# A two-layer transformer block on one core: mean of squares ahead of the input sums, head squares in smaller pieces, fifth product in another bank

## Time and profile before

| | us |
|---|---|
| median of three runs | 1791.35 (1790.88 to 1792.32) |
| profiled execution | 1793.69 |
| its span, first to last instruction | 1792.0 |
| PE busy | 1772.9 (99%) |
| DVE busy | 1279.3 (71%) |
| ACT busy | 895.0 (50%) |
| POOL busy | 140.7 (8%) |
| mean granted TensorE clock, share of full | 0.996 |

### The profile page before, as it was taken

One profiled execution on the slowest core, in us unless ns is written; L12 is line 12 of the kernel. 1 busy time (PEld: TensorE's weight loads), 2 busy tenths in 40 slices (PEclk: granted clock), 3 DMA queues, 4 the chain that ended last, 5 costly groups with the idle time before them and its releaser, 6 DMA issues.

```text
span 1792.0 us, 26289 instructions
## 1 busy us (share of the span) xinstructions
PE 1772.9 (99%) x8791; PEld 1500.4 (84%) x8791; DVE 1279.3 (71%) x1689; ACT 895.0 (50%) x1248; POOL 140.7 (8%) x190
## 2 busy tenths in 40 slices
PE   9999999999999999999999999899999999999999
PEld 7888888888888888888888887677888888888887
DVE  6567777556898788878877868887888655555654
ACT  7434444446455455545544556566544455554442
POOL 1012121000001000000000000110003011000000
PEclk9999999999999999999999999999999999999999
DMA  9564545555568667766775676455655655555554
GB/s 331 201 218 158 169 159 176 183 170 188 177 208 237 196 192 213 232 186 191 217 234 187 201 230 203 139 187 188 200 187 177 199 176 177 175 176 188 188 188 153
DMA packets 99116, 347.30 MB, mean 194 GB/s; under 512 B 11472, under 2 KB 11872, under 8 KB 98656
## 3 DMA queue, kind: packets, MB, share of 16 engines
q1 hardware_dynamic: 93392, 333.23, 57.0%
q0 software_dynamic: 4784, 12.60, 3.3%
q10 hardware_dynamic: 864, 0.44, 0.1%
HBM read 336.77 MB, written 2.11 MB: 189 GB/s over the span
## 4 chain that ended last, share of the span: by engine, by line
PE 90%; DVE 4%; ACT 3%; issue 2%; DMA 2%; POOL 0%; SPq 0%; ACTq 0%; DVEq 0%; POOLq 0%
PE bank L472 30%; PE bank L451 23%; PE bank L456 12%; PE bank L766 6%; PE bank L768 6%; PE bank L767 6%; DMA raw<-in_stream 2%; ACT w_hi L978 2%; DVE w_lo L1486 1%; PE bank L522 1%; PE bank L488 1%; ACT gate L1366 1%; PE bank L644 1%; PE bank L659 1%; PE bank L601 0%
## 5 line engine op out<-in xcount | busy, mean ns | idle before, releaser
L1486 DVE TENSOR_TENSOR w_lo<-raw,w_hi 128x1024 fp32r<-128x1024 f32 x620 | 754.5, 1226 | 386.7 <-ACT w_hi L978 382.9
L978 ACT ACTIVATE w_hi<-raw 128x1024 fp32r<-128x1024 f32 x620 | 648.2, 1055 | 590.1 <-PE bank L472 263.2
L451 PE MATMUL bank<-h_both,w_hi 128*128 128x512 f32 x1792 | 432.9, 394 | 0.5 <-DVE gate L1894 0.5
L451 PEld LDWEIGHTS bank<-h_both,w_hi 128*128 128x128 f32 x1792 | 330.3, 188 | 66.5 <-issue 0.9
L472 PE MATMUL bank<-w_hi,h_both 128*128 128x512 f32 x1160 | 362.8, 394 | 0.0
L472 PEld LDWEIGHTS bank<-w_hi,h_both 128*128 128x128 f32 x1160 | 216.5, 189 | 43.7
L456 PEld LDWEIGHTS bank<-h_both,w_lo 128*128 128x128 f32 x1792 | 229.8, 191 | 8.7
L456 PE MATMUL bank<-h_both,w_lo 128*128 128x256 f32 x1792 | 232.5, 283 | 0.0
L472 PE MATMUL bank<-w_lo,h_both 128*128 128x512 f32 x580 | 226.6, 391 | 0.0
L472 PE MATMUL bank<-w_hi,a_both 128*128 128x512 f32 x576 | 178.5, 391 | 0.0
L472 PEld LDWEIGHTS bank<-w_lo,h_both 128*128 128x128 f32 x580 | 109.2, 188 | 23.3
(11 more groups left out here) (278 smaller groups left out, 1793.6 us busy)
## 6 DMA issues: line engine op xcount, KB each, us to landing
raw<-in_stream SPq DMA_DIRECT2D x622, 512.0 KB, 3.5
wide<-scaled POOLq DMA_DIRECT2D x21, 256.0 KB, 4.7
res<-in_x SPq DMA_DIRECT2D x4, 512.0 KB, 7.3
rowg<-in_norm_rows POOLq DMA_DIRECT2D x2, 1024.0 KB, 8.9
gate<-cum_rows POOLq DMA_DIRECT2D x1, 2048.0 KB, 7.2
out<-wide SPq DMA_DIRECT2D x8, 256.0 KB, 3.7
wide<-gate POOLq DMA_DIRECT2D x7, 256.0 KB, 8.4
gate<-in_x_turned SPq DMA_DIRECT2D x5, 256.0 KB, 6.4
```

The lines of the kernel that those rows point to most:

```text
L451: pe.matmul(tile_sum[b][:, :], w_hi[:, slot + half, k * P:(k + 1) * P], h_both[:, 8 * half + k, :], start=half == 0 and k == 0, stop=False)
L978: nc.scalar.activation(w_hi[:, slot, :], raw[:, slot, :], ACT.Copy).then_inc(hi_ready, 1)
L1486: nc.vector.tensor_tensor(w_lo[:, slot, :], raw[:, slot, :], w_hi[:, slot, :].bitcast(F32), ALU.subtract).then_inc(lo_ready, 1)
```

## The change

- **MLP's end (DVE).** The first four of six `ff_gain` stand ahead of the remainder of chunk 59, that remainder and the one of chunk 60 follow, and then the last two gains.
- **v_b (DVE, ACT).** `scale_of_rows(2)` stands ahead of all input sums, `diagonal(3)` behind the second round. Each of the three rounds has a buffer of its own, in the space of `h_part[1]` to `h_part[3]`; their splits by ACT come later in its order (two splits of weights behind), and the three subtractions of DVE come together at the end.
- **q, k (ACT).** `scale_qkv` is cut into pieces: per block two pieces with two squares each and one with the scaling, twelve per group. Two of them at a time follow the splits 0, 2, 3, 6, 7 and 10.
- **PSUM banks (PE).** The `seven` banks are reordered, so that p5 lands in the bank which the next group takes last. PE waits for two joining sums (`8 * w + 2`) at the start of a group, and for all four where it first writes that bank.

```diff
 h_part = [gate_flat[:, 2048 + n * 512:2560 + n * 512] for n in range(4)]
+h_raw = [h_part[q + 1].rearrange("p (f t) -> p f t", f=4) for q in range(STEPS)]
 h_sum = [gate_flat[:, 2048 + b * 256:2304 + b * 256] for b in range(2)]
 qkv_forms = Forms(in_a("h_w_raw", 0, [3, GROUP_COLS], F32)[:, :, :], in_a("h_w_hi", 1536, [3, GROUP_COLS]),
-                  in_a("h_w_lo", 3072, [3, GROUP_COLS]), in_a("h_x_raw", 7680, [4, P], F32)[:, :, :],
+                  in_a("h_w_lo", 3072, [3, GROUP_COLS]), h_raw,
                   in_a("h_x_hi", 4608, [STEPS, 4, P]), in_a("h_x_lo", 6144, [STEPS, 4, P]), h_part)
...
-seven_bank = [plain_bank[1], plain_bank[0]]
+seven_bank = [[bank[2], bank[5], bank[3], bank[4]], plain_bank[0]]
 h_bank = [[bank[2], bank[3], bank[7], bank[6]], [bank[0], bank[1], bank[5], bank[4]]]
+h_seven = [[bank[0], bank[4], bank[1], bank[5]], [bank[2], bank[6], bank[3], bank[7]]]
...
     def joined(w):
-        pe.wait_ge(join_step, 8 * w + 4)
+        pe.wait_ge(join_step, 8 * w + 2)
+    def fifth_read(w):
+        return lambda: pe.wait_ge(join_step, 8 * w + 4)
     def wide_group(g, n):
         c = FIRST["mlp"] + g * 64 + 32 + 16 * n
         w = 2 * g + n
         plain, seven = plain_bank[n], seven_bank[n]
-        if w:
+        if n == 1:
             joined(w - 1)
+        elif g:
+            fifth_read(w - 1)()
...
-                wide_chunk(c, j + k, 2 * pair + k, plain, (a_hi, a_lo), tiles_read if n == 0 else {})
+                wide_chunk(c, j + k, 2 * pair + k, plain, (a_hi, a_lo),
+                           tiles_read if n == 0 else {3: fifth_read(w - 1)})
...
-        plain, seven = h_bank[i % 2], h_bank[1 - i % 2]
+        plain, seven = h_bank[i % 2], h_seven[i % 2]
...
-                           {} if i else {3: lambda: pe.wait_ge(rows_ready, 2)})
+                           {3: fifth_read(w - 1) if i else lambda: pe.wait_ge(rows_ready, 2)})
...
+    def h_forms_hi(q):
+        act.wait_ge(x_form_step, 4 * STEPS * FF_GROUPS + 6 * q + 6)
+        nc.scalar.activation(qkv_forms.x_hi[:, q, :, :], qkv_forms.x_raw[q], ACT.Copy).then_inc(x_form_hi_ready, 1)
     for m in range(4):
         norm_block(2, 8 + m)
         next_split(c + 4 + m)
...
         res_square(2, 2 * m + 1)
     for m in range(4):
         next_split(c + 8 + m)
-        if m < STEPS:
-            act.wait_ge(x_form_step, 4 * STEPS * FF_GROUPS + 6 * m + 6)
-            nc.scalar.activation(qkv_forms.x_hi[:, m, :, :], qkv_forms.x_raw, ACT.Copy).then_inc(x_form_hi_ready, 1)
+        if m >= 2:
+            h_forms_hi(m - 2)
+    h_forms_hi(2)
...
-    def scale_qkv(i, t):
-        for n in range(2):
-            block = 2 * t + n
+    def qkv_squares(i, block, half):
+        t, n = divmod(block, 2)
+        if half == 0:
             act.wait_ge(join_step, 8 * (WIDE_GROUPS + i) + block + 5)
-            if i < 2:
-                if 4 * i + block >= 2:
-                    act.wait_ge(qkv_sq, 4 * i + block - 1)
-                for head in range(4):
-                    ins = nc.scalar.activation(gelu_a[:, n, head * P:(head + 1) * P],
-                                               h_part[block][:, head * P:(head + 1) * P], ACT.Square,
-                                               scale=rstd[:, t:t + 1],
-                                               accum_out=head_sq[:, t, i * 8 + 4 * n + head:i * 8 + 4 * n + head + 1])
-                ins.then_inc(qkv_sq, 1)
-            start = i * 1024 + n * GROUP_COLS
-            nc.scalar.activation(qkv[:, t, start:start + GROUP_COLS], h_part[block], ACT.Copy,
-                                 scale=rstd[:, t:t + 1]).then_inc(qkv_in, 1)
+            if 4 * i + block >= 2:
+                act.wait_ge(qkv_sq, 4 * i + block - 1)
+        for head in range(2 * half, 2 * half + 2):
+            at = i * 8 + 4 * n + head
+            ins = nc.scalar.activation(gelu_a[:, n, head * P:(head + 1) * P],
+                                       h_part[block][:, head * P:(head + 1) * P], ACT.Square,
+                                       scale=rstd[:, t:t + 1], accum_out=head_sq[:, t, at:at + 1])
+        if half == 1:
+            ins.then_inc(qkv_sq, 1)
+    def qkv_scale(i, block):
+        t, n = divmod(block, 2)
+        act.wait_ge(join_step, 8 * (WIDE_GROUPS + i) + block + 5)
+        start = i * 1024 + n * GROUP_COLS
+        nc.scalar.activation(qkv[:, t, start:start + GROUP_COLS], h_part[block], ACT.Copy,
+                             scale=rstd[:, t:t + 1]).then_inc(qkv_in, 1)
+    def qkv_part(i, at):
+        block, piece = divmod(at, 3)
+        if piece < 2:
+            qkv_squares(i, block, piece)
+        else:
+            qkv_scale(i, block)
+    parts_after = {0: (0, 1), 2: (2, 3), 3: (4, 5), 6: (6, 7), 7: (8, 9), 10: (10, 11)}
     act.wait_ge(vb_sums, 4)
     for i in range(QKV_WIDE):
         for j in range(0 if i else RING, WIDE_CHUNKS):
-            wide_split(c + 16 + 16 * i, WIDE_GROUPS + i, j, qkv_forms, h_bank[1 - i % 2])
-            if i and j < 2:
-                scale_qkv(i - 1, j)
-    for t in range(NT):
-        scale_qkv(QKV_WIDE - 1, t)
+            wide_split(c + 16 + 16 * i, WIDE_GROUPS + i, j, qkv_forms, h_seven[i % 2])
+            if i:
+                for at in parts_after.get(j, ()):
+                    qkv_part(i - 1, at)
+    for block in range(4):
+        qkv_scale(QKV_WIDE - 1, block)
...
     add_group(g, 2, 0)
-    rest(c + 55, 3)
     dve.wait_ge(rowg_in, 32)
-    for n in range(3):
+    for n in range(2):
         for t in range(NT):
             ff_gain(n, t)
-    rests(c + 56, range(RING))
+    rest(c + 55, 3)
+    rest(c + 56, 0)
+    for t in range(NT):
+        ff_gain(2, t)
+    rests(c + 56, range(1, RING))
...
+        if q:
+            dve.wait_ge(x_form_step, done)
...
     dve.wait_ge(chunk_done, c)
     next_rest(c + 8)
+    scale_of_rows(2)
     h_forms(0)
     next_rest(c + 9)
-    scale_of_rows(2)
-    h_forms_lo(0)
     h_forms(1)
     next_rest(c + 10)
-    h_forms_lo(1)
+    diagonal(3)
     h_forms(2)
     next_rest(c + 11)
-    h_forms_lo(2)
-    diagonal(3)
+    for q in range(STEPS):
+        h_forms_lo(q)
     nc.vector.tensor_scalar(half_rstd[:, :], rstd[:, :], 0.5, None, ALU.mult).then_inc(half_rstd_ready, 1)
...
```

More of the change, by code:

```diff
@@ L1326, in vb_split @@
                 else:
-                    wide_split(c + 16, WIDE_GROUPS, j, qkv_forms, h_bank[1])
+                    wide_split(c + 16, WIDE_GROUPS, j, qkv_forms, h_seven[0])
             for n in range(2):
@@ L2016, in h_forms @@
                 a12, a22 = [h_sum[1][:, t * P:(t + 1) * P] for t in range(NT)]
-                s1, s2, s3, s4 = [qkv_forms.x_raw[:, f, :] for f in range(4)]
+                s1, s2, s3, s4 = [qkv_forms.x_raw[q][:, f, :] for f in range(4)]
                 dve.wait_ge(x_form_step, done + 2)
@@ L2028, in h_forms_lo @@
                 dve.wait_ge(x_form_hi_ready, STEPS * FF_GROUPS + q + 1)
-                nc.vector.tensor_tensor(qkv_forms.x_lo[:, q, :, :], qkv_forms.x_raw,
+                nc.vector.tensor_tensor(qkv_forms.x_lo[:, q, :, :], qkv_forms.x_raw[q],
                                         qkv_forms.x_hi[:, q, :, :].bitcast(F32),
@@ L2092, in _ @@
                               (lambda t, n: qkv_drain(i - 1, t, n)) if i and q == 0 else None)
-                wide_join(c + 16 + 16 * i, WIDE_GROUPS + i, h_bank[1 - i % 2], h_part)
+                wide_join(c + 16 + 16 * i, WIDE_GROUPS + i, h_seven[i % 2], h_part)
             for t in range(NT):
```

## The result

The changed kernel takes 1776.65 us (median of 4 runs, 1776.46 to 1777.32), the kernel before beside it 1791.84 us (4 runs, 1790.88 to 1794.12): a ratio of 0.9914, 95% interval 0.9897 to 0.9931. The forecast was 1776.1, range 1773 to 1781. A ratio can differ by up to 0.0005 from the quotient of the two medians given beside it. One later execution of the kernel before took 1951.83 us at a mean granted clock of 0.85; it is left out of every figure. The profiled execution took 1777.32 us with a span of 1775.6; that of before 1793.69 and 1792.0.

The account below looks back on a forecast made before the run. TensorE was taken as busy 1772.9 of 1792.0 us, so only its waits and slow clock could be won. Terms -1.2 - 9.0 + 3.1 - 8.2 = -15.3 us gave 1776.1 us for the median, range 1773.0 to 1781.0.

Parts of the forecast that it names:

- Gains: End of the MLP: moving the last two gains behind two remainders removes PE's wait at the half chunks, -1.2 us.
- a shorter MLP: Sign of being wrong: the prediction said the MLP's length doesn't move.
- The ones product: v_b stage: PE no longer waits for DVE's diagonal before the products with the matrix of ones, -9.0 us.
- the two rivals against it: v_b stage: diagonal still comes after 1133.8, 1782.0 us, 3%; or nothing won there, the term's bound of 0.
- The lag: First wide q, k, v group: PE waits for DVE's v_b chain at a remainder and the first weight form, +3.1 us.
- rival 1: First wide group: the clock falls behind the new lag too, 1.7 us more, 1777.8 us; chance 21%.
- rival 2: First wide group: no new lag, DVE's chain shrinks as much as PE's, 1773.0 us; chance 11%.
- rival 3: First wide group: larger lag of 5.5 us as stream landings come under the chain, 1778.5 to 1780; chance 9%.
- The collision with POOL: v_b chain: POOL's causal-weights instruction still slows a DVE one, now the remainder of chunk 13; 0.9 us kept.
- Squares: Second and third wide groups: shorter bursts of ACT's head squares remove both 2.2 us waits of PE, -8.2 us.
- The slower rival: Wide groups: six bursts of squares instead of two stand in front of splits, 17.2 us lost, 1793.3 us; chance 3%.
- Banks: Wide groups: taking the fifth product's bank last wins nothing, value 0, bounds 0 and -0.5 us.

Follow-up runs that it names:

- the half kernels: Two kernels, each the kernel before with half the v_b change: DVE's new order alone, ratio 0.9995; a buffer per pair with later splits and subtractions, ratio 0.9967.
- the long wait put back: The changed kernel with nine added DVE subtractions of 128x384 between the last x form and v_b's first multiplication: 1780.64 us.
- moved whole: The kernel before with the squares of two blocks in one piece, behind splits 3 and 7 instead of 0 and 1: 1784.43 us, ratio 0.9958.
- the first experiments: Four kernels, each the kernel before with one part alone: head squares 1785.27 us, mean of squares and buffers 1784.14, gains 1790.78, banks 1792.27.

## Why the prediction was right

**Gains**, -1.2: the place gave 1.2 us (1.89 us between the two products of the earlier trace rows before, 0.68 now). Up to chunk 48 the two profiles agree to 0.03 us (1045.23 and 1045.26), so this is all that the MLP lost; the prediction's list of signs, which calls a shorter MLP one of being wrong, forgot this term of its own. Alone it is worth nothing that the runs can tell.

**The ones product**, -9.0: measured 8.94, from the last product ahead of the matrix (1133.58 before, 1132.40 after) to the wide group (1148.65 and 1138.53). Right for its reason, and the two rivals against it (diagonal still late, no gain) are out. It held two things in one, and the half kernels separate them: the reorder hides the wait, the freed waits of DVE win most of the time. Some luck is in the size: from the last product to the wide group the five profiles with the long wait have 14.37 to 15.58 us (15.07 before), so against another of them the term would have come out at 8.2 to 9.5 us.

**The lag**, +3.1: measured +2.0. It stood where it was said to stand, a piece at a remainder and the rest at the form (0.41 and 1.35 us, forecast 1.6 and 1.7). From the start of DVE's chain to the form the forecast was 20.9 us and the trace has 20.80. The lag is 2.2 instead of 3.3 us since that chain began earlier: the remainder ahead of the reduce came 1.67 us earlier than before, not 1.2 (0.5 us; in the profile of before ACT's split upstream had waited 0.68 us for a DMA), and from the reduce to the chain DVE took 11.70 us, where the prediction has 12.2 (0.5 us: about half of it its seams at the three waits, which were counted as work, and 0.16 a shorter collision with POOL). That is the one mis-sized term, 1.1 us.

**The clock behind the lag** (rival 1, 21%): it stayed at 1.00, so the rival is out for this kernel. Its condition was not tested by itself: with the long wait put back, the clock fell ahead of the form, where it cost nothing, and held behind the form, where rival 1 has it (1.00 from 1158 to 1162). No lag (rival 2) and the larger lag (rival 3) are out by the 15.83 us to the form.

**The collision with POOL** moved, as said, but not onto the remainder of chunk 13: it hit the last operation of the first round, 1.06 us instead of 0.29, one place earlier, since POOL's selection began at 1123.23, when that operation was next. The remainder behind it took its usual 1.21 us. The price was right (0.8 against 0.9 us), and taking POOL away gave 0.77 us back. By the rule of the Trainium skill (SBUF — State Buffer, Who interferes with whom) a VectorE instruction with two SBUF inputs contends with a GpSimd instruction that reads SBUF, and the one issued later is blocked. The traces agree: POOL's instruction of 1.13 us began first and ended at 1124.36, DVE's ended at 1124.51, and it is 0.29 us long without POOL's.

**Squares**, -8.2: measured -8.19 between the profiles. The remainder of chunk 6 was ready 3.3 us before PE wanted it; "nearly 4" was forecast. The slower rival needed bursts in front of splits with less than 1.4 us to spare, and there was no such split: counted by products, the least that a remainder or form had to spare in the second and third group was 2.3 us. But a median doesn't hold both clock falls that the profiled execution held. Each wait is worth 2.5 or 4.1 us, so the part is worth 5.0 to 8.2 us; alone it measured 5.5, and moved whole 6.8.

**Banks**, 0: nothing that can be told, alone.

**The sum** of the terms was -15.3 on the profiled execution. The tile behind the groups came 16.35 us earlier, and the whole execution was 16.37 us shorter: all of it lies in this stretch. The medians differ by 15.2; against the 23 runs of the kernel before in the first experiments it would be 14.1. The parts alone add up to 12.2 us by their medians (6.7, 5.5, 0, and nothing for the banks). The gap of 2 to 3 us is within what the intervals of the parts, 1.8 to 2.5 us to either side, leave open, and no kernel with two parts was run to look for its cause. That the median landed on the forecast within 0.6 us has some luck in it: the lag was 1.1 us smaller than forecast, and the step from the profiled run to the median, a plain shift of 2.3 us, took no account of the fact that part of the profiled run's surplus was clock falls, which the change removes. The changed kernel's profiled run is only 0.7 us above its median.

## What to carry to other kernels

When one engine's order is changed to meet a deadline, ask what its waiting time is made of: where rounds wait for one shared buffer, a reorder mostly hands the wait on, and a buffer for each round, with the dependent steps placed later, removes it. Then price what is late next by the length of the chain of the engine that sets it, start to end. Its length came out to 0.1 us here, its start was 1 us off, and what was put into that chain or taken out came back within 0.2 us in the length of the group or the lead of its start, as long as a lag was left. A profile of one execution may hold clock falls that the median does not, so a term that contains one is a range.

## What the runs showed of the hardware

- Behind a 2.2 us wait of PE in the same place the granted clock fell in 5 of 12 cases (0.79 in the mean of 8 us) and held in 7; it fell once behind 2.6 us, and in all five profiles with a wait of 6.3 to 6.8 us (0.65 to 0.80 from there to the wide group). Behind two waits of 0.4 and 1.35 us, 3 us apart, it held. The difference is 1.6 us a case (45.6 against 44.0 us for a group). The runs of the kernel before lie between 1788.7 and 1794.1 us, those of the changed kernel within 0.9 us. The mean granted clock recorded for each of 55 runs of the kernel before goes with the time: 1792.4 us on average in the 17 runs at 0.996, 1790.7 in the 21 at 0.997, 1790.1 in the 17 at 0.998; the four of the changed kernel have 1.00. Which fall makes the difference in a run, one behind a 2.2 us wait or a longer one behind the ones product, is not shown.
- A diagonal (an instruction with one matrix and one scalar per row) took longer beside POOL's selection as well: in the kernel with the buffers alone the two took 1.30 us beside it, 0.48 us in the changed kernel without. This is one instance.

```profile
1134.68 1.30 DVE L1561 TENSOR_SCALAR qk_norm<-ident,rstd 128x128 f32<-128x128 f32 x2
```

```profile
1134.62 1.09 POOL L2392 TENSOR_SCALAR_AFFINE_SELECT gate<-gate 128x1024 f32<-128x1024 f32 x1
```
